# Alternating two streams of row gathers, one by one in place of four and four

## The chip, the cores and the metric

The kernel runs on one core of a Trainium2 chip. The metric is the device time of one execution in microseconds; a time quoted for a kernel is the median of its runs, and a profile shows one execution.

## What is computed

One layer of a hybrid decoder on 512 prompt tokens and 8 decode tokens: a modulated norm, one wide input projection, sliding-window attention with sinks, a pooling mixer, gated branches and an output projection; then a product-key retrieval of experts. The change touches only the last part:

```python
def peer_ffn(h, w_q, sub_keys, u_tab, v_tab):
    ...                       # 8 heads: top 16 of 128 x 128 keys -> 128 (expert, gate) pairs a token
    def block(args):          # 128 tokens a block
        hb, eb, gb = args
        act = jax.nn.gelu(jnp.einsum('td,thkd->thk', hb, u_tab[eb]))
        return jnp.einsum('thk,thkd->td', gb * act, v_tab[eb])
    ...
```

Each token needs 128 rows of the table u and 128 rows of the table v, of 1024 float32 each. Row numbers depend on the data.

## The kernel before

The program has one instruction stream for each engine, with semaphores between them written out by hand. Up to about 600 us it does the mixer, the attention and the projections; from there to the end it does the expert part, whose first steps still lie beside the query projection and the routing.

The prompt is 4 blocks (NB) of 128 tokens, one token on each partition. A block has 128 slots, four of them (GS) a step: 32 steps (STEPS) a block, 128 in all, each numbered n. One gather on POOL (an indirect DMA, L459) fetches for one slot one row for each of the 128 tokens, 512 KB, on POOL's DMA queue. A step needs four gathers of u rows and four of v rows:

- **u.** When all four have landed, DVE runs four multiply-and-sum reductions (L946) of u rows with h, adds one to `u_used`, and after ACT's GELU (L606) multiplies with the gates (L951). ACT scales four diagonal matrices by these coefficients (L610).
- **v.** When all four have landed and the diagonals are ready, PE adds eight products of a diagonal with half a tile of v rows into two banks of psum; in float32 each shows as two matmuls, so a step is 16 matmuls of L1338. Then it adds one to `v_used`.

u rows and v rows have eight buffers each, two sides of four; step n uses side n % 2. POOL may issue u of step n when DVE is done with step n-2, and v of step n when PE is done with step n-2 (L456; the counters begin at AHEAD = 2). Each side of each table has one landing semaphore, which counts all four gathers. POOL's loop (L464 to L474) issues the four u gathers of step n and then the four v gathers of step n-1. Everything that POOL issues goes in program order, and a wait holds all that is behind it. Other waits in this loop (`routed`) are for the row numbers.

DVE also routes block b+1 between the steps of block b (top-k, index arithmetic). A last part does the 8 decode tokens with 16 more gathers (L481).

Of the kernel before, what the change touches and what calls it, by code (L numbers as in the profile page):

```python
# [30 lines left out]
NB = T // P  # L31
# [20 lines left out]
GS = 4  # L52
# [119 lines left out]
def decoder_layer(nc, x_prompt, x_sample, cache_k, cache_v, state_pool, c_prompt, c_sample, norm1_g,  # L172
                  norm2_g, w_ada, b_ada, w_in, q_norm_g, k_norm_g, attn_sinks, w_pool, pool_scale,
                  w_branch_attn, w_branch_pool, w_out, peer_wq, peer_subkeys, peer_u, peer_v, consts,
                  y_prompt, y_sample, k_win_p, v_win_p, pool_p, k_win_s, v_win_s, pool_s):
    plan = bank_plan()
    order = {key: i for i, (key, _) in enumerate(plan)}
    taker = dict(plan)
    turn = {}
# [6 lines left out]
    content_before = [max((j for j in range(i) if bank_of[j] == bank_of[i]), default=None) for i in range(len(plan))]  # L186
    chunks = weight_chunks()
    chunk_at = {key: i for i, (key, _) in enumerate(chunks)}

    def sem(name):  # L190
        return nc.alloc_semaphore(name)
# [15 lines left out]
    u_landed = [sem(f"u_landed_half{i}") for i in range(2)]  # L207
    v_landed = [sem(f"v_landed_half{i}") for i in range(2)]
# [4 lines left out]
    u_used, v_used = sem("u_used"), sem("v_used")  # L213
# [8 lines left out]
    def at(off, n, a=None):  # L222
        v = arena[:, off:off + n]
        return v if a is None else v.rearrange("p (a b) -> p a b", a=a)

    def take(n):
        top[0] += n
        assert top[0] <= AR, top[0]
        return top[0] - n
# [63 lines left out]
    eidx = at(take(NB * SLOTS), NB * SLOTS, NB).bitcast(I32)  # L293
# [26 lines left out]
    u_rows = [at(o_ring + i * D, D) for i in range(2 * GS)]  # L320
    v_rows = [at(o_ring + (2 * GS + i) * D, D) for i in range(2 * GS)]
# [8 lines left out]
    def wait_filled(eng, key):  # L330

        eng.wait_ge(bank_filled, order[key] + 1)
# [15 lines left out]
    STEPS = SLOTS // GS  # L348
# [9 lines left out]
    def _(sp):  # L358
# [14 lines left out]
        for i, (key, _) in enumerate(chunks):  # L373
            if i >= RING:
                wait_filled(sp, chunks[i - RING][1])
            r = ring[i % RING]
            wide = r.rearrange("p (k n) -> p k n", k=8)
            if key[0] == "ada":
                src, dst = wad[:, :, key[1] * 512:(key[1] + 1) * 512], wide
            elif key[0] in starts:  # L380
                c0, n = starts[key[0]]
                src, dst = win[:, :, c0:c0 + n], wide[:, :, 0:n]
            elif key[0] == "gate":
                c0 = 1280 + key[1] * 512
                src, dst = win[:, :, c0:c0 + 512], wide
            elif key[0] == "wo":
                src, dst = w_out[0].rearrange("(k p) n -> p k n", p=P)[:, :, key[1] * 512:(key[1] + 1) * 512], wide
            elif key[0] == "wb":
                src, dst = w_branch_pool[0].rearrange("(k p) n -> p k n", p=P), r.rearrange("p (k n) -> p k n", k=4)
            else:  # L390
                dst = r.rearrange("p (k n) -> p k n", k=4)
                for kv in range(KV):
                    half = w_branch_attn[0, kv * G * HD:(kv + 1) * G * HD, :].rearrange("(j e) n -> e j n", j=G)
                    sp.dma_start(dst[kv * HD:(kv + 1) * HD], half).then_inc(w_loaded[i % RING], 8 * 2)
                continue
            sp.dma_start(dst, src).then_inc(w_loaded[i % RING], 16)
# [21 lines left out]
    @block.gpsimd  # L418
    def _(pool):
        pool.dma_start(gqk[:, 0, :], q_norm_g[0:1, :].broadcast_to((P, HD))).then_inc(small_loaded, 16)  # L420
        pool.dma_start(gqk[:, 1, :], k_norm_g[0:1, :].broadcast_to((P, HD))).then_inc(small_loaded, 16)
        pool.dma_start(sinks, attn_sinks[0:1, :].broadcast_to((P, HEADS))).then_inc(small_loaded, 16)
        for kv in range(KV):
            pool.dma_start(sinks4[0:G, kv:kv + 1],
                           attn_sinks[0, kv * G:(kv + 1) * G].rearrange("(j o) -> j o", o=1), allow_slow_non_contiguous=True).then_inc(small_loaded, 16)
        pool.dma_start(wpool, w_pool[0].rearrange("g c e -> c g e")).then_inc(small_loaded, 16)
        pool.dma_start(k0[0:S, :], cache_k[0, :, 0].rearrange("b h e -> b (h e)")).then_inc(small_loaded, 16)
        pool.dma_start(kc[:, P:], consts[:, P:]).then_inc(consts_loaded, 16)

        pool.wait_ge(qk_normed, 1)  # L430
        pool.dma_start(k_win_p[0, 0].rearrange("t h e -> t (h e)"), zqk[:, NB - 1, 512:640]).then_inc(windows_stored, 16)  # L431
        pool.dma_start(v_win_p[0, 0].rearrange("t h e -> t (h e)"), zv[:, NB - 1, :]).then_inc(windows_stored, 16)
        pool.dma_start(pool_p[0, 0], zp[P - HIST:P, NB - 1, :]).then_inc(windows_stored, 16)

        wait_filled(pool, ("d", 1))
        pool.dma_start(pext[0:HIST * S, :], state_pool[0].rearrange("b r c -> r b c")).then_inc(tail_loaded, 16)
        pool.dma_start(pext[HIST * S:P, :], zp[0:S, NB, :]).then_inc(tail_loaded, 16)
        pool.wait_ge(tail_loaded, 32)
        pool.dma_start(pool_s[0].rearrange("b r c -> r b c"), pext[S:P, :]).then_inc(windows_stored, 16)

        wait_filled(pool, ("gate", 2 * C - 1, 1))
        for cache, tile, new in ((cache_k, ktile, zqk[0:S, NB, 512:640]), (cache_v, vtile, zv[0:S, NB, :])):
            pool.dma_start(tile[0:WIN - 1], cache[0, :, 1:WIN].rearrange("b s h e -> s b (h e)")).then_inc(cache_loaded, 16)  # L443
            pool.dma_start(tile[WIN - 1:WIN], new).then_inc(cache_loaded, 16)
        pool.wait_ge(cache_loaded, 64)
        pool.dma_start(k_win_s[0].rearrange("b s h e -> s b (h e)"), ktile).then_inc(windows_stored, 16)
        pool.dma_start(v_win_s[0].rearrange("b s h e -> s b (h e)"), vtile).then_inc(windows_stored, 16)
        wait_filled(pool, ("y", PG - 1, 1))
        pool.dma_start(v0[0:1], cache_v[0:1, :, 0].rearrange("o b h e -> o b (h e)")).then_inc(oldest_v_loaded, 16)
        pool.wait_ge(merged_ready, 2 * C)  # L450
        pool.dma_start(sk_rows, peer_subkeys[0].rearrange("h c n e -> n (h c) e")).then_inc(subkeys_loaded, 16)  # L451
        wait_filled(pool, ("ada", 11))
        def gather(table, buf, used, landed, n):

            b, k, side = n // STEPS, n % STEPS, n % 2
            pool.wait_ge(used, n + 1)  # L456
            for i in range(GS):
                slot = k * GS + i
                pool.indirect_dma_start(  # L459
                    out=buf[side * GS + i], out_offset=None, in_=table[0],  # L460
                    in_offset=bass.IndirectOffsetOnAxis(ap=eidx[:, b, slot:slot + 1], axis=0),
                ).then_inc(landed[side], 16)

        for n in range(NB * STEPS):  # L464
            if n < OVER * TURN and n % TURN == 0:
                pool.wait_ge(routed, n // TURN + 1)
            elif n == OVER * TURN:
                pool.wait_ge(routed, OVER + 1)
            elif n == EARLY * TURN:
                pool.wait_ge(routed, OVER + 2)  # L470
            gather(peer_u, u_rows, u_used, u_landed, n)
            if n:
                gather(peer_v, v_rows, v_used, v_landed, n - 1)
        gather(peer_v, v_rows, v_used, v_landed, NB * STEPS - 1)  # L474

        pool.wait_ge(sample_routed, 1)
        for table, buf, used, landed in ((peer_u, u_rows, u_used, [sample_u_landed[t // GS] for t in range(S)]), (peer_v, v_rows, v_used, sample_v_landed)):
            for q in range(2):
                pool.wait_ge(used, AHEAD + NB * STEPS - 1 + q)
                for t in range(q * GS, (q + 1) * GS):  # L480
                    pool.indirect_dma_start(out=buf[t], out_offset=None, in_=table[0],  # L481
                                            in_offset=bass.IndirectOffsetOnAxis(ap=idx_s[:, t:t + 1], axis=0)).then_inc(landed[t], 16)
        pool.wait_ge(windows_stored, 16 * 6)
# [965 lines left out]
```

## Time and profile before

| | us |
|---|---|
| median of 3 runs (2167.91 to 2173.15) | 2167.99 |
| profiled execution | 2177.73 |
| its span, first to last instruction | 2175.9 |
| DVE reductions, L946, 512 | 597.8 |
| POOL gathers of u, L459, 512 | 664.2 |
| POOL gathers of v, L459, 512 | 494.2 |
| PE matmuls, L1338, 2048 | 1043.7 |

Engines: PE is TensorE, PEld its weight loads, DVE is VectorE, ACT is ScalarE, POOL is GpSimd. "arena" is the one tensor that holds all of the core's on-chip memory. A row of the **timeline** has the start in us, the duration in us, engine, line, operation, what it writes and reads, how many instructions are merged in the row and, in brackets, the idle time before it with what ended it; "issue" means that nothing in the profile was waited for. A row of **waits** has engine and line, what was waited for, and the sum in us, the number and the longest of these waits. A row of **windows** has the stretch, its length, each engine's busy time with its number of instructions, then the granted share of PE's full clock, the DMA engines' busy share and GB/s. A row of **lines** groups instructions: count, busy us, mean ns of one, and the idle time before them.

### The profile page before, as it was taken

What the parts mean: (1) busy time and instruction counts of PE and PEld (TensorE: products, weight loads), DVE (VectorE), ACT (ScalarE), POOL (GpSimd) and SP (SyncE); (2) the same over time, 40 slices, a digit from 0 to 9 for tenths busy, and PEclk for the clock granted to TensorE, in tenths of its full rate; (3) what the DMA queues carried; (4) which work ended last, traced back from release to release, by engine and by line L of the source; (5) the groups of instructions that cost most, each with busy time, mean ns of one, the idle gap of its engine ahead of it and who ended that gap; (6) DMA issues with size and microseconds to landing.
All of it is one profiled execution on the core that took longest, in us unless ns stands there. A gap on an engine that the chain in (4) does not pass through costs nothing.

```text
span 2175.9 us, 16338 instructions
## 1 busy us (share of the span) xinstructions
PE 1705.3 (78%) x4907; PEld 881.3 (41%) x4907; DVE 1077.1 (50%) x2685; ACT 369.0 (17%) x988; POOL 1200.8 (55%) x1066
## 2 busy tenths in 40 slices
PE   6999990999989997777676666776776777777778
PEld 2458740868556653223222222322332332223222
DVE  3012210423356678885665565665566565443443
ACT  2013430101122111111111111111111111111111
POOL 0000011000055557777777777777777778777774
PEclk9999995899999998898989899889888888988999
DMA  8222142032289889999999999999999999999996
GB/s 297 78 78 81 48 98 78 20 135 78 87 310 328 303 283 372 354 371 360 370 370 352 361 364 356 374 367 354 362 361 370 356 359 348 365 357 356 372 357 266
DMA packets 196404, 612.37 MB, mean 281 GB/s; under 512 B 21808, under 2 KB 39508, under 8 KB 196218
## 3 DMA queue, kind: packets, MB, share of 16 engines
q0 software_dynamic: 155216, 551.61, 68.7%
q1 hardware_dynamic: 41130, 60.04, 8.4%
q8 instruction: 30, 0.49, 0.1%
q14 instruction: 28, 0.23, 0.0%
HBM read 607.78 MB, written 3.59 MB: 281 GB/s over the span
## 4 chain that ended last, share of the span: by engine, by line
POOL 48%; PE 31%; issue 16%; DMA 3%; DVE 2%; ACT 0%; SPq 0%; DVEq 0%; ACTq 0%; POOLq 0%
POOL arena L459 48%; PE psum L1090 18%; PE psum L1338 4%; PE psum L1152 4%; DMA arena<-arena 1%; DMA arena<-in_peer_v,arena 1%; DMA arena<-in_x_sample 1%; POOL arena L443 1%; PE psum L1416 1%; PE psum L1322 1%; ACT arena L492 0%; PE psum L1179 0%; DVE arena L946 0%; PE psum L1405 0%; PE psum L1251 0%
## 5 line engine op out<-in xcount | busy, mean ns | idle before, releaser
L1338 PE MATMUL psum<-arena 128*128 128x512 f32 x2048 | 1043.7, 668 | 377.6 <-DMA arena<-in_peer_v,arena 368.3
L459 POOL DMA_INDIRECT arena<-in_peer_u,arena x512 | 664.2, 1297 | 347.6 <-issue 151.7
L946 DVE CUSTOM_DVE_ANT_0 arena<-arena 128x1024 f32<-128x1024 f32 x512 | 597.8, 1222 | 468.5 <-DMA arena<-in_peer_u,arena 467.6
L1338 PEld LDWEIGHTS psum<-arena 128*128 128x128 f32 x2048 | 426.8, 214 | 983.2 <-issue 868.0
L459 POOL DMA_INDIRECT arena<-in_peer_v,arena x512 | 494.2, 965 | 159.5 <-issue 155.7
L1090 PE MATMUL psum<-arena 128*128 128x260 f32 (+2 forms) x1812 | 449.2, 408 | 10.9 <-ACT arena L492 8.0
L1090 PEld LDWEIGHTS psum<-arena 128*128 128x128 f32 (+1 forms) x1812 | 320.2, 180 | 129.5 <-issue 78.5
L610 ACT ACTIVATE arena<-arena 128x128 f32<-128x128 f32 x512 | 163.5, 390 | 267.1 <-DVE arena L951 267.1
L606 ACT ACTIVATE arena<-arena 128x4 f32<-128x4 f32 x128 | 26.3, 205 | 901.8 <-DVE arena L946 901.8
L492 ACT ACTIVATE arena<-psum 128x512 f32<-128x512 f32 (+9 forms) x181 | 76.1, 451 | 498.4 <-PE psum L1090 286.6
L431 POOL DMA_DIRECT2D out<-arena x1 | 0.6, 561 | 179.5 <-DVE arena L745 179.5
L1152 PE MATMUL psum<-arena 128*128 128x512 f32 (+3 forms) x240 | 88.6, 530 | 1.6 <-DVE arena L708 1.6
L1152 PEld LDWEIGHTS psum<-arena 128*128 128x128 f32 (+1 forms) x240 | 40.9, 172 | 48.5 <-issue 44.0
L962 DVE COPY arena<-psum 128x512 f32<-128x512 f32 x16 | 11.0, 690 | 73.4 <-PE psum L1322 73.2
L756 DVE SCALAR_TENSOR_TENSOR arena<-psum,arena 128x512 f32<-128x512 f32 (+1 forms) x16 | 9.2, 619 | 70.2 <-PE psum L1179 70.0
L1241 PE MATMUL psum<-arena 128*128 128x128 f32 x8 | 2.0, 428 | 51.1 <-DMA arena<-arena 51.1
L946 DVE DVE_READ_ACCUMULATOR2_ANT arena<- 128x1 f32 x512 | 41.5, 81 | 0.0
L451 POOL DMA_DIRECT2D arena<-in_peer_subkeys x1 | 1.2, 1172 | 71.9 <-DVE arena L818 71.9
L443 POOL DMA_DIRECT2D arena<-in_cache_k x1 | 6.7, 6696 | 60.3 <-PE psum L1201 60.3
L688 DVE TENSOR_TENSOR arena<-psum,arena 128x36 f32<-128x36 f32 x12 | 2.4, 196 | 75.2 <-PE psum L1116 75.2
L951 DVE TENSOR_TENSOR arena<-arena 128x4 f32<-128x4 f32 x128 | 21.2, 166 | 35.9 <-issue 17.9
L858 DVE FIND_INDEX8 arena<-arena 128x8 uint32<-128x128 f32 (+3 forms) x99 | 32.6, 329 | 0.0
(197 smaller groups left out, 817.6 us busy)
## 6 DMA issues: line engine op xcount, KB each, us to landing
arena<-in_w_ada SPq DMA_DIRECT2D x12, 2048.0 KB, 8.9
arena<-in_w_in SPq DMA_DIRECT2D x6, 2048.0 KB, 7.7
arena<-in_peer_u,arena POOLq DMA_INDIRECT x520, 6.2
arena<-in_peer_v,arena POOLq DMA_INDIRECT x520, 6.2
arena<-in_peer_wq SPq DMA_DIRECT2D x16, 512.0 KB, 8.9
arena<-in_w_out SPq DMA_DIRECT2D x2, 2048.0 KB, 13.7
arena<-in_x_prompt SPq DMA_DIRECT2D x4, 512.0 KB
arena<-in_w_branch_attn SPq DMA_DIRECT2D x2, 1024.0 KB, 20.6
```

What stands on the lines that cost most here:

```text
L443: pool.dma_start(tile[0:WIN - 1], cache[0, :, 1:WIN].rearrange("b s h e -> s b (h e)")).then_inc(cache_loaded, 16)
L459: pool.indirect_dma_start(out=buf[side * GS + i], out_offset=None, in_=table[0], in_offset=bass.IndirectOffsetOnAxis(ap=eidx[:, b, slot:sl ...
L492: ins = act.activation(out, in_, f, **kw)
L606: act.activation(gelus[:, side, :], acts[:, side, :], ACT.Gelu_apprx_tanh).then_inc(gelu_done, 1)
L610: ins = act.activation(diags[:, side * GS + i, :], ident, ACT.Copy, scale=coefs[:, side, i:i + 1])
L858: dve.max_index(i[:, 0:8], v[:, 0:8], s)
L946: ins = dve.tensor_tensor_reduce(rows_i, rows_i, h2n[:, b, :], 1.0, 0.0, ALU.mult, ALU.add, acts[:, side, i:i + 1])
L1090: ins = pe.matmul(out, a, b, start=(n == 0), stop=(n == len(pairs) - 1))
L1152: ins = pe.matmul(o, hT[:, k, cols(b)], wt[:, k, 0:n], start=(k == 0), stop=(k == C - 1))
L1322: ins = pe.matmul(o[:, b * P:(b + 1) * P], pq[:, m % 2, b * P:(b + 1) * P], skT[m], start=True, stop=True)
L1338: ins = pe.matmul(psum[:, 2 * (b % 2) + h, :], diags[:, side * GS + i, :], v_rows[side * GS + i][:, h * 512:(h + 1) * 512], start=False, s ...
L1416: ins = pe.matmul(psum[0:S, 4 + h, :], coef_s[:, t * S:(t + 1) * S], v_rows[t][:, h * 512:(h + 1) * 512], start=(t == 0), stop=(t == S - 1 ...
```

## The change

POOL's loop issues the same gathers with the same waits in another order: u gather i of step n and v gather i of step n-1 in turn, i from 0 to 3. The wait for u's buffers stands ahead of the first u gather, the wait for v's buffers now ahead of the first v gather, which is the second gather of the step. The last iteration has v gathers alone.

```diff
-        def gather(table, buf, used, landed, n):
-
-            b, k, side = n // STEPS, n % STEPS, n % 2
-            pool.wait_ge(used, n + 1)
-            for i in range(GS):
-                slot = k * GS + i
-                pool.indirect_dma_start(
-                    out=buf[side * GS + i], out_offset=None, in_=table[0],
-                    in_offset=bass.IndirectOffsetOnAxis(ap=eidx[:, b, slot:slot + 1], axis=0),
-                ).then_inc(landed[side], 16)
-
-        for n in range(NB * STEPS):
+        def gather(table, buf, landed, n, i):
+
+            slot = n % STEPS * GS + i
+            pool.indirect_dma_start(
+                out=buf[n % 2 * GS + i], out_offset=None, in_=table[0],
+                in_offset=bass.IndirectOffsetOnAxis(ap=eidx[:, n // STEPS, slot:slot + 1], axis=0),
+            ).then_inc(landed[n % 2], 16)
+
+        for n in range(NB * STEPS + 1):
...
-            gather(peer_u, u_rows, u_used, u_landed, n)
-            if n:
-                gather(peer_v, v_rows, v_used, v_landed, n - 1)
-        gather(peer_v, v_rows, v_used, v_landed, NB * STEPS - 1)
+            if n < NB * STEPS:
+                pool.wait_ge(u_used, n + 1)
+            for i in range(GS):
+                if n < NB * STEPS:
+                    gather(peer_u, u_rows, u_landed, n, i)
+                if n and i == 0:
+                    pool.wait_ge(v_used, n)
+                if n:
+                    gather(peer_v, v_rows, v_landed, n - 1, i)
```

## Rows read from the trace of the kernel before

**Rows 1.** The page: the chain that ended last, share of the span by engine.

```profile
POOL 48%; PE 31%; issue 16%; DMA 3%; DVE 2%; ACT 0%; SPq 0%; DVEq 0%; ACTq 0%; POOLq 0%
```

**Rows 2.** Waits of POOL, 881 to 2104 us (all of them).

```profile
POOL arena L459 <- issue: 256.2, 841, 0.3
```

**Rows 3.** Windows, 881.19 to 2091.62 us, POOL.

```profile
881.19:2091.62 1210.43, 956.98 (x832) 0.89 0.97 362
```

**Rows 4.** Timeline of POOL, 1490 to 1520 us: gathers of u and of v.

```profile
1495.11 0.94 POOL L459 DMA_INDIRECT arena<-in_peer_v,arena  x1 [0.30 <-issue]
...
1501.52 0.94 POOL L459 DMA_INDIRECT arena<-in_peer_u,arena  x1 [0.30 <-issue]
...
1507.75 1.76 POOL L459 DMA_INDIRECT arena<-in_peer_u,arena  x1 [0.30 <-issue]
1509.81 1.98 POOL L459 DMA_INDIRECT arena<-in_peer_u,arena  x1 [0.31 <-issue]
1512.10 0.94 POOL L459 DMA_INDIRECT arena<-in_peer_u,arena  x1 [0.30 <-issue]
...
1514.59 0.94 POOL L459 DMA_INDIRECT arena<-in_peer_v,arena  x1 [0.30 <-issue]
...
1519.57 0.94 POOL L459 DMA_INDIRECT arena<-in_peer_u,arena  x1 [0.30 <-issue]
```

**Rows 5.** Lines of POOL, 881 to 2104 us: gathers by table.

```profile
L459 POOL DMA_INDIRECT arena<-in_peer_u,arena x421 | 572.5, 1360 | 128.3 <-issue 128.3
L459 POOL DMA_INDIRECT arena<-in_peer_v,arena x420 | 395.9, 943 | 127.9 <-issue 127.9
```

**Rows 6.** Timeline of DVE, 1507 to 1515 us: one step's reductions and its coefficients.

```profile
1507.47 1.23 DVE L946 CUSTOM_DVE_ANT_0 arena<-arena 128x1024 f32<-128x1024 f32 x1 [3.73 <-DMA arena<-in_peer_u,arena]
...
1508.62 1.22 DVE L946 CUSTOM_DVE_ANT_0 arena<-arena 128x1024 f32<-128x1024 f32 x1
...
1510.91 1.22 DVE L946 CUSTOM_DVE_ANT_0 arena<-arena 128x1024 f32<-128x1024 f32 x1
...
1514.76 0.17 DVE L951 TENSOR_TENSOR arena<-arena 128x4 f32<-128x4 f32 x1 [0.26 <-issue]
```

**Rows 7.** Timeline of PE, 910 to 2130 us: steps, the first and the last.

```profile
910.10 7.13 PE L1338 MATMUL psum<-arena 128*128 128x512 f32 x16 [2.72 <-DMA arena<-in_peer_v,arena]
...
1502.11 8.82 PE L1338 MATMUL psum<-arena 128*128 128x512 f32 x16 [3.74 <-DMA arena<-in_peer_v,arena]
1512.64 7.13 PE L1338 MATMUL psum<-arena 128*128 128x512 f32 x16 [1.71 <-DMA arena<-in_peer_v,arena]
...
2096.70 8.83 PE L1338 MATMUL psum<-arena 128*128 128x512 f32 x16 [4.72 <-DMA arena<-in_peer_v,arena]
...
2120.70 9.02 PE L1338 MATMUL psum<-arena 128*128 128x512 f32 x16 [5.11 <-DMA arena<-in_peer_v,arena]
```

**Rows 8.** Line L459, 881 to 2104 us: from a gather's issue to its landing.

```profile
DMA to landing us min/median/max: 5.1/6.2/8.9
```

**Rows 9.** Timeline of ACT, 1510 to 1520 us: one step's diagonals.

```profile
1514.96 1.28 ACT L610 ACTIVATE arena<-arena 128x128 f32<-128x128 f32 x4 [2.58 <-DVE arena L951]
```

**Rows 10.** Timeline of POOL, 2095 to 2150 us: the last step's first v gather.

```profile
2129.99 1.27 POOL L459 DMA_INDIRECT arena<-in_peer_v,arena  x1 [3.82 <-PE psum L1338]
```

**Rows 11.** Windows of 5 us, POOL: clock, DMA share, GB/s.

```profile
1497.00:1502.00 5.00, 4.09 (x4) 1.00 1.03 419
1502.00:1507.00 5.00, 3.78 (x5) 0.66 0.95 350
...
1512.00:1517.00 5.00, 3.76 (x4) 1.00 0.90 311
```

**Rows 12.** Windows, 700 to 800 us, PE, PEld, DVE, ACT and POOL.

```profile
700.00:800.00 100.00, 100.00 (x382) 66.49 (x381) 67.56 (x191) 18.58 (x53) 49.63 (x52) 1.00 0.87 304
```

**Rows 13.** Waits of POOL, 600 to 881 us.

```profile
POOL arena L459 <- DVE arena L946: 63.0, 13, 9.9
```

## The prediction

> **What bounds the kernel now.** I read the page first: POOL leads the chain that ended last, with 48% of the span at L459, the line that issues the gathers, and another 16% is "issue"; PE has 31% [rows 1]. L459 does its work after 600 us, so the second view is what POOL waited for in the long stage that repeats, between 881 and 2104 us: nothing. 841 gaps sum to 256.2 us, none longer than 0.3 us [rows 2]: the engine's own gap between two gathers. POOL issues back to back and sets the pace. From 881.19 to 2091.62 it issues 832 gathers, 104 steps of eight, in 1210.43 us [rows 3]: 11.64 us per step.
>
> A gather costs 0.94 us and the gap 0.30 us, 1.245 us between starts [rows 4], so eight cost 9.96 us. The other 1.68 us per step is gathers that last longer: in the grouped view u gathers average 1360 ns and v gathers 943 ns [rows 5], which is (421 x 0.42 + 420 x 0.003)/105 = 1.69 us per step. The timelines show why. At 1507.75 a u gather takes 1.76 us and the next, at 1509.81, 1.98 us [rows 4]; in these microseconds DVE runs the four reductions of L946, from 1507.47, one every 1.145 us [rows 6]. Take 0.94 us off each gather's end and it could go on at 1508.57 and 1510.85, just where the second and the fourth reduction begin. So a gather that starts while a reduction runs is held to that reduction's end. One that follows the last reduction takes 0.94 us [rows 4].
>
> How far is the rest from taking over? A step's buffers come free again when DVE (u) or PE (v) has worked on the step two before it. The last v gather of one step starts at 1495.11 [rows 4], PE begins that step at 1502.11 (7.00 us later) and works 8.82 us, to 1510.93 [rows 7]; the gather that reuses the buffers starts at 1514.59 [rows 4]. **Slack: 3.66 us.** For u: last gather 1501.52 [rows 4], reductions 1507.47 to 1512.13 [rows 6], reuse at 1519.57 [rows 4], 7.4 us. Both cover POOL now. The two slacks are what the change spends.
>
> **The change, part by part.** It removes and adds no gather, no byte and no instruction on another engine. POOL's program has the same waits, with the v wait in another place.
>
> (1) *The order of issue.* Now, from the last u gather of a step to the first u gather that reuses the buffers there are thirteen places in POOL's queue (v v v v, u u u u, v v v v, u); afterwards ten (v, a whole step of eight, u). For v the same: thirteen (u4 v4 u4, then v) becomes ten (a whole step, u, v). The other gap, from the first to the last gather of one table in a step, grows from three places to six.
>
> (2) *The u wait.* Ten places: 10 x 1.245 + 1.69 (one step's holds) = 14.14 us. Needed: landing (median 6.2 us from issue [rows 8]), four reductions 4.66 us [rows 6], about 0.3 us for release: 11.2 us. It still fits, with 3 us to spare. Cost nothing; the cover is those 3 us. The later u rows also reach PE later through the coefficients. From a last u gather at 1501.52 [rows 4] the coefficients start at 1514.76 [rows 6] and ACT ends its four scalings at 1516.24 [rows 9]: 14.7 us. From the last u to the last v of a step there will be nine places, 9 x 1.245 + 1.69 = 12.9 us, plus the landing: 19.1 us. v rows still come last. Nothing.
>
> (3) *The v wait.* Ten places again, 14.14 us, against 19.48 us in the example [rows 4] (thirteen places and two steps' holds; 19.57 us by the means). The slack shrinks by 5.43 us. It is needed for landing, PE's step and 0.27 us of release (PE's step from 2120.70 ends at 2129.72 [rows 7], the waiting gather starts at 2129.99 [rows 10]: the one place where POOL is held by PE today). PE's steps between the first and the last row of [rows 7] are of three kinds: of 104, 46 take 7.13 us, 38 take 8.5 to 8.83, and 20 take 9 or more, up to 10.2. The difference is the clock, 0.89 on the mean there [rows 3]: in the step from 1502.11, which PE began after 3.74 us of idle time and needed 8.82 us for [rows 7], the granted share is 0.66 from 1502 to 1507; in the 7.13 us step from 1512.64, after 1.71 us of idle time [rows 7], it is 1.00 [rows 11]. The two levels are 1.2 and 2.4 GHz, and the lower one follows the longer idle time. Read as in the example, slack averages 5.96, 4.29 and 3.22 us in the three kinds. Less 5.43: **+0.53, -1.14 and -2.21 us.** POOL will stand at the first v gather after every PE step that ran partly at the low clock. Behind that wait are queued three u gathers and the whole rest of the step, so DVE and the DMA queue get everything later.
>
> (4) *The sum.* 38 x 1.14 + 20 x 2.21 = 88 us if every shortfall counted in full; with those of the fast steps that fall short, 89. Two things take some back. A stall also moves the next step's first v gather, whose own PE step was issued before it: going through the 104 steps in order, with each stall deducted from the next step's shortfall, leaves 72 us. And while POOL stands, the DMA queue drains, so the next rows land sooner: landing spans 5.1 to 8.9 us, median 6.2 [rows 8]. I take 0.4 us, about a third of the way from median to minimum (an estimate): the same pass with 5.03 us in place of 5.43 gives about 55 us, **0.53 us per step.** Bounds of this term: 30 us (1.1 us sooner, the minimum landing), 89 us (nothing given back).
>
> (5) *Elsewhere.* Before about 780 us PE is the bound (busy 100.00 of 100 us from 700 to 800 [rows 12]); POOL waits there for DVE, 63.0 us in 13 waits [rows 13], and a later u row or an earlier v wait lies in that idle time. From 800 to 881 DVE has a backlog from routing; a stall of POOL is again covered by rows that landed early. 0, at most 5 us. The tail keeps its order (v rows of the last step alone), 0 to 2 us. I take 0 for both.
>
> Sum: 55 us. The profiled run took 2177.73 us (span 2175.9), which would become about 2233; against the median of 2167.99 it is 2223 us.
>
> **The rivals.** *A, same time.* Memory would be the limit, and order is then free. The stage moves 362 GB/s on the mean at a DMA share of 0.97 [rows 3], so little seems to be left; the time would stay 2168. Against it: from 1497 to 1502, after a run of gathers that nothing held, the rate is 419; from 1512 to 1517, after two held ones, 311 [rows 11]. The rate follows POOL, not the other way round. The Trainium skill ("DMA: Bandwidth & Descriptors", Specifications) puts the HBM limit of one core at about 358 GB/s; by that rule the stage would be full and A the likeliest, but the trace's 419 GB/s in 5 us differs from it, and the measurement decides. Half of A's chance is another road to the same end: the slow steps of PE follow each other, so that stalls are mostly given back, the landing comes down to its minimum, and holds shrink by what is left. 2168.
>
> *B, faster.* The holds shrink. A step's holds depend on when, after DVE's first reduction, POOL's next gather starts: at 0.28 us (1507.75 against 1507.47 [rows 4, 6]) they are 0.82 + 1.04. Started at about 1.1 us only one hold of 1.04 would be left, 0.65 us less per step, 68 us over 105 steps. Together with the stalls of (4): 2168 + 55 - 68 = 2155. It decides only if nearly every step shifts to that best phase: holds must fall by more than 0.53 + 0.06 us per step. Against it: in the cyclic order of eight, the gather that meets the reductions stays the fifth after a step's last u gather, and the landing of that gather sets DVE's start in both versions. The phase has no reason to improve.
>
> *C, much slower.* POOL's stalls lengthen PE's idle time, and every PE step runs at the low clock in its first half: 10.1 us. Then two steps need landing 6.1 + 10.1 + 0.27 + six places from first to last v gather (6 x 1.245 + 1.69 = 9.16) = 25.6 us, 12.8 per step, +1.17 us: 2168 + 123 = 2291. For it: low clock follows idle time, which is 4.7 to 5.1 us before the 8.83 and 9.02 us steps at the end [rows 7]. Against: the idle share grows only by half a microsecond in 11.6.
>
> That the order is not what it says can hardly be: POOL issues in program order on one queue, as the rows of today show four and four [rows 4].
>
> **How the numbers follow.** Forecast (v turnaround stalls POOL, +20 to +94 us) 0.70; C 0.08; A 0.10; B 0.12. A measurement of this kernel tells about 0.3% (6.5 us) from no change. Slower by more than that: 0.70 + 0.08 = 0.78; within: 0.10; faster: 0.12. Range: low 2165, just under A; high 2262, all 89 us of (4) and 5 us of (5); B and most of C, 0.2, are left out.
>
> **What would show it.** In the changed profile, POOL's waits must show a new row, L459's successor waiting for PE L1338, in some 40 to 60 of the 105 steps, about 1 us each, and no row for DVE L946 after 881 us beyond a few. Gathers of both tables should be long in equal parts, with holds still near 1.7 us per step. u and v landings should be a little under 6.2 us, and the DMA rate about 345 GB/s. PE's idle time before L1338 should grow by some 50 us. I am wrong if POOL waits for PE almost nowhere (then slack (3) is misread), or if it waits but holds fall as much (B).

## The result, and the profile after

The changed kernel takes 2273.52 us (median of 4 runs, 2271.14 to 2283.51) against 2168.37 us: a ratio of 1.0488, 95% interval 1.0454 to 1.0523, 105 us slower. The forecast was 2223, the range 2165 to 2262. The sign came as forecast, and so did the place of the new wait; the size was about twice the forecast one.

The page of the changed kernel, its chain (share of the span by engine), to be read against [rows 1]. Line numbers moved: the gathers are L456, the reductions L948, PE's products L1340.

```profile
PE 52%; POOL 20%; DMA 18%; issue 9%; ACT 1%; DVE 0%; SPq 0%; ACTq 0%; DVEq 0%; POOLq 0%
```

POOL had 48% and PE 31%. The chain now leads from POOL through a landing to PE and back to POOL: 18% of it is DMA, which had 3%. What POOL waits for between 881 and 2200 us, against [rows 2]:

```profile
POOL arena L456 <- issue: 240.6, 789, 0.3
POOL arena L456 <- PE psum L1340: 126.8, 58, 3.8
```

The second row is new. Each such wait contains the 0.30 us gap that every gather has, so POOL stands (waits beyond that gap) 126.8 - 58 x 0.30 = 109 us. The same 104 steps in one window, against [rows 3]:

```profile
887.16:2181.28 1294.12, 933.26 (x832) 0.85 0.93 338
```

A step went from 11.64 to 1294.12/104 = 12.44 us, and the rate from 362 to 338 GB/s. The gathers by table, against [rows 5]:

```profile
L456 POOL DMA_INDIRECT arena<-in_peer_v,arena x423 | 485.1, 1147 | 238.2 <-PE psum L1340 126.8 <-issue 111.3
L456 POOL DMA_INDIRECT arena<-in_peer_u,arena x424 | 466.4, 1100 | 129.3 <-issue 129.3
```

Holds, the time by which gathers last longer than 0.94 us, now fall on both tables: (485.1 + 466.4 - 847 x 0.94)/106 = 1.47 us a step, 0.22 less than before.

Where the time went, by the two profiled executions (spans 2269.3 and 2175.9, 93.4 us apart): up to the first u gather of step 21 it is 887.16 - 881.19 = 6.0 us, in the 104 steps 1294.12 - 1210.43 = 83.7, behind them (2269.3 - 2181.28) - (2175.9 - 2091.62) = 3.7. The medians differ by 105 and not by 93, since the profiled execution of before lay 9.4 us above its median and that of after 2.4 below its own.

Three steps on PE, and POOL at the same time, show the pattern. PE's timeline:

```profile
1563.12 9.93 PE L1340 MATMUL psum<-arena 128*128 128x512 f32 x16 [7.62 <-DMA arena<-in_peer_v,arena]
1573.34 7.13 PE L1340 MATMUL psum<-arena 128*128 128x512 f32 x16 [0.29 <-DMA arena<-in_peer_v,arena]
1589.46 8.71 PE L1340 MATMUL psum<-arena 128*128 128x512 f32 x16 [8.99 <-DMA arena<-in_peer_v,arena]
```

POOL's timeline:

```profile
1573.32 1.82 POOL L456 DMA_INDIRECT arena<-in_peer_v,arena  x1 [3.52 <-PE psum L1340]
...
1585.21 0.94 POOL L456 DMA_INDIRECT arena<-in_peer_v,arena  x1 [0.30 <-issue]
...
1598.44 1.92 POOL L456 DMA_INDIRECT arena<-in_peer_v,arena  x1 [2.18 <-PE psum L1340]
```

And the granted clock in the first two of these steps (windows; the share of the full clock is the third number from the end):

```profile
1563.00:1573.30 10.30, 9.93 (x16) 0.72 1.02 409
1573.30:1580.50 7.20, 7.13 (x16) 1.00 0.55 168
```

PE ends at 1573.05, and 0.27 us later the gather that stood for 3.2 us starts. The step that follows begins 0.29 us after the last one, at full clock, takes 7.13 us, and its gather at 1585.21 waits for nothing. The one after that starts after 8.99 us of idle time and takes 8.71 us; POOL stands again, at 1598.44. In 56 of 104 steps POOL stands, mostly every second one.

### The profile page after: what moved, and what is told of

Read it like the earlier page. It is cut to its first block, busy times and chain, and to the rows that moved or that the text cites. A ratio compares the mean times of both kernels' runs of the same rounds, so it can differ in the third digit from the quotient of the medians.

```text
span 2269.3 us, 16338 instructions
## 1 busy us (share of the span) xinstructions
PE 1717.5 (76%) x4907; PEld 888.0 (39%) x4907; DVE 1078.7 (48%) x2685; ACT 368.9 (16%) x988; POOL 1177.2 (52%) x1066
## 4 chain that ended last, share of the span: by engine, by line
PE 52%; POOL 20%; DMA 18%; issue 9%; ACT 1%; DVE 0%; SPq 0%; ACTq 0%; DVEq 0%; POOLq 0%
PE psum L1340 26%; POOL arena L456 20%; PE psum L1092 18%; DMA arena<-in_peer_v,arena 16%; PE psum L1154 4%; DMA arena<-arena 1%; DMA arena<-in_x_sample 1%; POOL arena L443 1%; PE psum L1418 1%; PE psum L1324 1%; ACT arena L494 0%; PE psum L1181 0%; PE psum L1407 0%; PE psum L1253 0%; PE psum L1133 0%
## 5 line engine op out<-in xcount | busy, mean ns | idle before, releaser
L1340 PE MATMUL psum<-arena 128*128 128x512 f32 x2048 | 1057.8, 676 | 459.8 <-DMA arena<-in_peer_v,arena 447.9
L948 DVE CUSTOM_DVE_ANT_0 arena<-arena 128x1024 f32<-128x1024 f32 x512 | 598.1, 1223 | 565.6 <-DMA arena<-in_peer_u,arena 564.6
L1340 PEld LDWEIGHTS psum<-arena 128*128 128x128 f32 x2048 | 433.9, 218 | 1072.3 <-issue 923.9
L456 POOL DMA_INDIRECT arena<-in_peer_u,arena x512 | 557.0, 1088 | 343.8 <-issue 151.9
L456 POOL DMA_INDIRECT arena<-in_peer_v,arena x512 | 577.9, 1129 | 282.8 <-PE psum L1340 148.2
L948 DVE DVE_READ_ACCUMULATOR2_ANT arena<- 128x1 f32 x512 | 41.5, 81 | 0.0
```

The source lines that it names most:

```text
L456: pool.indirect_dma_start(out=buf[n % 2 * GS + i], out_offset=None, in_=table[0], in_offset=bass.IndirectOffsetOnAxis(ap=eidx[:, n // STEP ...
L948: ins = dve.tensor_tensor_reduce(rows_i, rows_i, h2n[:, b, :], 1.0, 0.0, ALU.mult, ALU.add, acts[:, side, i:i + 1])
L1340: ins = pe.matmul(psum[:, 2 * (b % 2) + h, :], diags[:, side * GS + i, :], v_rows[side * GS + i][:, h * 512:(h + 1) * 512], start=False, s ...
```

## The experiments

My theory after the result: POOL stands because v's turn-around (landing, the whole PE step, release) no longer fits into the ten places of its queue. The rivals: alternation itself costs (mixed or later landings); and, for the size, that the clock feeds back.

| kernel | us | ratio to the kernel before, run beside it, 95% interval |
|---|---|---|
| changed kernel | 2273.52 | 1.0454 to 1.0523 |
| wait moved alone, four and four | 2230.38 | 1.0225 to 1.0273 |
| alternating, release by row | 2171.03 | 0.9980 to 1.0016 |
| alternating, six fillers | 2246.97 | 1.0303 to 1.0347 |
| alternating, three fillers | 2261.35 | 1.0384 to 1.0454 |
| eleven places | 2206.11 | 1.0131 to 1.0168 |
| twelve places | 2168.88 | 0.9974 to 1.0015 |
| nine places | 2407.98 | 1.1069 to 1.1122 |
| four and four, release by row | 2170.11 | 0.9992 to 1.0021 |
| the same, h from psum in 48 steps | 2099.68 | 0.9654 to 0.9697 |
| alternating, release by row, h from psum | 2103.65 | 0.9675 to 0.9720 |

**The wait without the alternation.** The order of before, with the v wait moved forward (the edit is shown against the changed kernel):

```diff
 for i in range(GS):
     if n < NB * STEPS:
         gather(peer_u, u_rows, u_landed, n, i)
     if n and i == 0:
         pool.wait_ge(v_used, n)
-    if n:
-        gather(peer_v, v_rows, v_landed, n - 1, i)
+for i in range(GS if n else 0):
+    gather(peer_v, v_rows, v_landed, n - 1, i)
```

> The four and four order of the kernel before; only the wait for v's buffers is put behind the first u gather, where the changed kernel has it. From the last v gather of a step to the wait there are again ten places, and six more from the gather behind the wait to the next last v gather, as in the changed kernel. Theory (the place of the v wait and PE's turn-around cost the time, not the alternation): about the changed kernel's 2273 us, 2255 to 2290, with some 55 waits of POOL for PE that sum to 105 to 130 us. Rival (alternation itself costs: later and mixed landings, other holds): 2165 to 2185.

It took 2230 us: 59 us slower than before with no alternation at all, but 43 less than I expected. POOL's waits between 881 and 2160 us:

```profile
POOL arena L456 <- PE psum L1340: 109.9, 64, 4.1
```

That is 109.9 - 64 x 0.30 = 91 us of standing, near the changed kernel's 109. What differs is where POOL stands. POOL's timeline and, below it, DVE's:

```profile
1419.80 1.01 POOL L456 DMA_INDIRECT arena<-in_peer_u,arena  x1 [0.30 <-issue]
1422.80 1.84 POOL L456 DMA_INDIRECT arena<-in_peer_u,arena  x1 [1.99 <-PE psum L1340]
```

```profile
1420.31 1.22 DVE L948 CUSTOM_DVE_ANT_0 arena<-arena 128x1024 f32<-128x1024 f32 x1 [0.32 <-DMA arena<-in_peer_u,arena]
1421.46 1.22 DVE L948 CUSTOM_DVE_ANT_0 arena<-arena 128x1024 f32<-128x1024 f32 x1
```

POOL stands up to 1422.80 while the reductions run, in which its gathers would in part have been held anyway. Added up over both timelines, 90 of 91 us of standing lie inside reductions here, and 13 of 109 in the changed kernel. Holds fall accordingly, to 1.28 us a step (from 1.69, 43 us over 105 steps): 91 - 43 = 48 us in the stage, and about 10 us more ahead of it. Standing that lies wholly inside the reductions still costs about half. So a stall's price is what is left after the holds it covers; both my theory and its rival had missed that.

**Release by row.** PE adds to `v_used` after each row's two products, and POOL waits for one row (the other waits on `v_used`, scaled by four, are left out):

```diff
-    if n and i == 0:
-        pool.wait_ge(v_used, n)
     if n:
+        pool.wait_ge(v_used, (n - 1) * GS + i + 1)
         gather(peer_v, v_rows, v_landed, n - 1, i)
...
     for i in range(GS):
         for h in range(2):
             ins = pe.matmul(...)
-    ins.then_inc(v_used, 1)
+        ins.then_inc(v_used, 1)
```

> The changed kernel, in which PE adds to v_used after each row's two products (four times a step) and POOL waits before each v gather for that row's buffer alone; all other waits on v_used are scaled. The first v gather then needs landing 6.4 + a quarter of PE's step, 2.2, + 0.27 = 8.9 us of the 14 us that ten places take. Theory (the wait for the whole PE step): POOL no longer waits for PE, 8 x 1.245 + holds of 1.45 to 1.7 us give 11.4 to 11.65 us a step: 2145 to 2175. Rival (alternation itself): it stays over 2230.

2171 us, the time of before (interval 0.9980 to 1.0016), in full alternation. POOL's waits for PE between 881 and 2200 us are 55 of 0.3 us, the gap itself; below it the window of the 104 steps, 11.6 us each as before:

```profile
POOL arena L456 <- PE psum L1339: 16.8, 55, 0.3
```

```profile
881.68:2086.00 1204.32, 950.63 (x833) 0.89 0.97 364
```

The release by row alone changes nothing in the order of before (2170 us, under "The holds"). So the whole loss is the wait for the end of PE's step. Alternation, later u rows and mixed landings cost nothing that can be measured.

**Places.** Three more orders, with the v wait always ahead of the first v gather:

```diff
-u v u v u v u v     # changed kernel, ten places
+u u v u v u v v     # eleven
+u u u v u v v v     # twelve
+v u v u v u u v     # nine
```

> Order u u v u v u v v: v begins one place later than in the changed kernel, so eleven places, 1.245 us more, from a last v gather to the wait. Theory (shortfall against places): each of some 55 stalls of 1.88 us shrinks by up to 1.245 us, some vanish: 30 to 50 us of waits, 2185 to 2220. Rival (alternation itself, same amount of mixing): within 15 us of the changed kernel, 2258 to 2288.

> Order u u u v u v v v: twelve places from a last v gather to the wait, two more than in the changed kernel, 12 x 1.245 + 1.6 = 16.5 us. In the changed kernel a stalled step's turn-around was 6.45 + 9.14 + 0.27 = 15.9 us. Theory (shortfall against places): only PE steps of over 9.7 us fall short, by under 1 us each: waits below 15 us, 2168 to 2188. Rival (each place of alternation costs the same share, 35 us): about 2203.

> Order v u v u v u u v: nine places to the wait, one fewer than in the changed kernel, and seven from first to last v gather. Theory: POOL stands in nearly every pair of steps, and a pair lasts turn-around 15.9 + 7 x 1.245 + 1.45 = 26.0 us against the changed kernel's 24.8: 0.6 us more a step, 2315 to 2350. Rival (the loss is used up at ten places, a floor set by the landing): within 15 us of 2273.

POOL's waits for PE from 881 us, in eleven, twelve and nine places:

```profile
POOL arena L456 <- PE psum L1340: 52.1, 46, 3.6
```

```profile
POOL arena L456 <- PE psum L1340: 5.4, 6, 2.4
```

```profile
POOL arena L456 <- PE psum L1340: 233.9, 54, 6.1
```

Net of the gaps: 38, 4 and 218 us (with nine places seven more waits, about 29 us net, stand under "issue"); the times are 2206, 2169 and 2408. Thirteen, twelve, eleven, ten and nine places cost 0, 1, 35, 105 and 240 us against the runs of before beside them: a threshold, then a curve that gets steeper. Twelve and eleven came as the shortfall against places says. Nine took 58 us more than the top of its range. PE's timeline there:

```profile
1584.07 9.93 PE L1340 MATMUL psum<-arena 128*128 128x512 f32 x16 [8.75 <-DMA arena<-in_peer_v,arena]
1594.74 7.13 PE L1340 MATMUL psum<-arena 128*128 128x512 f32 x16 [0.74 <-DMA arena<-in_peer_v,arena]
1611.72 9.77 PE L1340 MATMUL psum<-arena 128*128 128x512 f32 x16 [9.85 <-DMA arena<-in_peer_v,arena]
```

PE's steps pair up more sharply: a long idle time, a step at the low clock in part, one right behind it. A pair lasts 27.3 us (1584.07 to 1611.72 is 27.7), where I had 26.0. The steps on which POOL waits average 9.5 us against the changed kernel's 9.1, and the release takes 0.78 us in place of 0.27 (1594.00 to 1594.78, the start of the gather that waited) there. In five of the seven waits under "issue" the gather starts 3.3 us after PE's end; why, and the rest, I have not taken apart.

**Fillers.** Matmuls of zeros ahead of PE's steps, to keep the clock up:

```diff
+for i in range(0 if isinstance(it, int) else 6):     # or 3
+    pe.matmul(psum[:, 2 * (b % 2) + i % 2, :], zeros, zeros[:, 0:1].broadcast_to((P, 512)),
+              start=False, stop=False, skip_group_check=True)
 pe.wait_ge(v_landed[side], ...)
```

> The changed kernel with six matmuls of zeros ahead of each PE step (from step 16 on), before its wait for v rows, so that PE is not idle long: 2.6 us at full clock. They add zero to the sums. Theory with a feedback through the clock (a stalled step is one that begins after 5.9 us of idle time at the low clock and takes 9.1 us): all steps take 7.13 us, the turn-around 6.4 + 7.13 + 0.27 = 13.8 us fits into ten places, the waits fall below 30 us in sum: 2165 to 2205. Rival (the clock is a by-product, the stalls come from late landing): steps shorten, waits stay above 70 us, 2230 or more.

> The changed kernel with three matmuls of zeros ahead of each PE step from step 16 on (1.3 us at full clock), in place of the six that themselves put PE's start off by 1 us. Theory (feedback through the clock): more PE steps of 7.13 us than the 40 of 104, start not put off, waits below 60 us: 2200 to 2250. Rival (the clock is a by-product): 2262 or more with the waits over 100 us.

2247 and 2261 us. The edit reaches less than both expectations say: a turn that is not part of a longer loop gets no fillers, and the trace has 1056 passes over zeros, twelve in each of 88 steps, from step 16 to 103. The last 24 steps ran without:

```profile
L1337 PE MATMUL psum<-arena x1056: 592/592/595, 856.5 to 1917.7; 128*128 128x512 f32 x176
```

The run with six could not tell the theories apart, because I had mispriced the filler. PE's timeline:

```profile
1499.65 5.33 PE L1337 MATMUL psum<-arena 128*128 128x512 f32 x12
1504.83 7.03 PE L1343 MATMUL psum<-arena 128*128 128x512 f32 x16
1511.69 5.33 PE L1337 MATMUL psum<-arena 128*128 128x512 f32 x12
1516.86 7.03 PE L1343 MATMUL psum<-arena 128*128 128x512 f32 x16
```

Six fillers are twelve float32 passes, 5.33 us: here PE never rests and is itself the bound, at 12.0 us a step. All 83 steps from 21 to 103 take 7.13 us, and POOL stands 41 us in them, where the changed kernel has 88. With three (2.7 us) 49 of these 83 steps take 7.13 us, against 32, and POOL stands 70 us; with the last steps it is 96 us against 109:

```profile
POOL arena L456 <- PE psum L1343: 112.0, 54, 3.9
```

2261 lies just under the rival's bound and just outside the theory's range. The interval (1.0384 to 1.0454) only touches the changed kernel's. So the clock has a share in the size, about 12 us by the medians, with a third of the slow steps gone where the fillers ran (34 left of 51); how much all of it is, these runs do not settle.

**The holds.** The release by row alone, in the order of before, and then with h read from psum in blocks 1 and 2 from their third turn on:

```diff
-ins = dve.tensor_tensor_reduce(rows_i, rows_i, h2n[:, b, :], ...)
+ins = dve.tensor_tensor_reduce(rows_i, rows_i, h_psum(b) if from_psum[0] else h2n[:, b, :], ...)
...
+act.wait_ge(y_ready, b)                  # ACT, after the block's first turn
+for i in range(2):
+    ins = act.activation(h_psum(b)[:, i * 512:(i + 1) * 512], h2n[:, b, i * 512:(i + 1) * 512], ACT.Copy)
+ins.then_inc(h_in_psum, 1)
...
+dve.wait_ge(h_in_psum, b)                # DVE, ahead of the third turn
+from_psum[0] = True
```

> The order of the kernel before with PE's release row by row and nothing else, the control for e8_rows_psum. POOL does not wait for PE in the kernel before, so nothing can be gained: 2162 to 2175. Rival (the release itself gave part of e8_rows_psum's 68 us): below 2155.

> The order of the kernel before, with PE's release row by row, and in blocks 1 and 2 from their third turn on (48 steps) the reductions read h from psum, where ACT copies it after the block before is finished, in place of the on-chip memory that POOL reads too. Theory (a gather is held while a reduction reads two operands from that memory): in these 48 steps gathers take 0.94 us, 8 x 1.245 = 9.96 us a step or 10.3 where the DMA queue sets the pace, against 11.64: 2168 - 48 x 1.34 = 2104, 2090 to 2125. Rival (the hold has another cause, any reduction): 2160 to 2180.

> The alternating order with PE's release row by row, and in blocks 1 and 2 from their third turn on h read from psum, as in e8_rows_psum, which has the four and four order (2099.7 us). In those 48 steps the DMA queue set the pace in e8_rows_psum: 410 GB/s, landing 9.3 us. Theory (order is free where the queue is full; u's turn-around of 9.3 + 4.66 + 0.3 = 14.3 us exceeds ten places, 12.45, but POOL's standing only drains the queue): 2095 to 2115. Rival (ten places bind u as they bound v): 48 steps x 0.9 us more, 2135 or above.

The control takes 2170 us, no change. With h in psum it is 2100 us, 3.2% faster than before and the best of all. POOL's timeline in that kernel, then DVE's:

```profile
1206.98 0.94 POOL L469 DMA_INDIRECT arena<-in_peer_u,arena  x1 [0.30 <-issue]
1208.22 0.94 POOL L469 DMA_INDIRECT arena<-in_peer_u,arena  x1 [0.30 <-issue]
1209.47 0.93 POOL L469 DMA_INDIRECT arena<-in_peer_v,arena  x1 [0.31 <-PE psum L1365]
1210.70 0.94 POOL L469 DMA_INDIRECT arena<-in_peer_v,arena  x1 [0.30 <-issue]
```

```profile
1207.30 1.22 DVE L966 CUSTOM_DVE_ANT_0 arena<-arena,psum 128x1024 f32<-128x1024 f32 x1 [3.20 <-DMA arena<-in_peer_u,arena]
1208.45 1.22 DVE L966 CUSTOM_DVE_ANT_0 arena<-arena,psum 128x1024 f32<-128x1024 f32 x1
1209.59 1.22 DVE L966 CUSTOM_DVE_ANT_0 arena<-arena,psum 128x1024 f32<-128x1024 f32 x1
```

The reductions last as long as before, and they hold no gather: in 44 such steps 345 of 352 gathers take up to 1.0 us, and the other seven, at most 1.27, lie beside a TENSOR_TENSOR of the routing on DVE. A stretch of block 1 and one of block 3, which still reads h from the on-chip memory (windows, POOL):

```profile
1150.00:1300.00 150.00, 112.92 (x121) 0.92 1.03 410
...
1850.00:2000.00 150.00, 118.39 (x104) 0.89 0.97 363
```

121 gathers in 150 us instead of 104, 410 GB/s instead of 363. The landing grows from 6.2 to 9.3 us (median): 121 gathers of 512 KB in 150 us ask for 423 GB/s and the queue moves 410, so it fills. But POOL still hardly stands: a step takes 10.04 us, where eight gathers with their gaps cost 9.96. So the queue does not yet set the pace. The alternating order costs little there (2104 us, the intervals overlap). The theory for that run gave the right time, but u's turn-around did not grow to 14.3 us, because the landing stayed near 7.6 us. It is 12.1 to 12.3 us and the release, about the 12.45 us of its ten places, and POOL stands some 8 us in 44 steps.

## Why the prediction was wrong in size

- **What bounds the kernel** stands: POOL back to back, with holds by the reductions. That was only read from the timelines; the kernel with h in psum shows it.
- **(1) and (2), order and u wait:** right. Between 881 and 2200 us POOL never waits for DVE, and releasing v by row, with u still at ten places, gives the time of before.
- **(3), the v wait:** right in place and count. Forecast were 40 to 60 waits of about 1 us for PE; there are 58, of 1.9 us net.
- **(4), the sum, is the step that failed.** 55 us of standing were forecast, 109 measured (105 of them behind the PE steps of the same 104). Three terms of it were mis-sized:
  - I took 0.4 us off for a queue that drains. In the changed kernel the landing to PE's start averages 6.45 us on the steps on which POOL waits, as before (6.48): six gathers have followed a stall by then. Without the 0.4 us the pass gives 73 us.
  - I named the release of 0.27 us in (3) and did not deduct it: slack ends at PE's end, the gather starts 0.27 later. With it the pass gives 85.
  - I kept the holds at 1.69 us inside the ten places. They fell by 0.22, so ten places without a stall take 13.9 us and not 14.14. With that the pass gives 95.

  The rule that a stall is credited to the next step did not fail. In the changed kernel's own timelines the shortfalls add up to 126 us, and 21 of them lie under the stall before; from the rows of before, with the release, the rule gives back 25. The last 10 us stay open. There are more slow steps, 64 of 104 in place of 58, but they are not longer (9.1 us on the mean in both). They are spread otherwise: on POOL's waits the PE step averages 9.1 us after 6.0 us of idle time, on the others 7.4 after 1.8. Only the runs with fillers bear on that, and they settle the clock's share no further than "some".
- **Holds, kept at 1.69 us:** they fell to 1.47, 23 us in the kernel's favour. The stage then loses 109 - 23 = 86 us, and 83.7 are measured. So fewer holds lengthen the standing and pay back more than that.
- **(5), elsewhere:** forecast 0, at most 7 us; it is 6.0 ahead of step 21 (12 waits for PE before 881 us, forecast as covered) and 3.7 behind. The other 12 us of the 105 are the two profiled executions' places against their medians, which no term of the sum could hold.
- **The range** ended at 2262 because "nothing given back" was taken as the worst case of a sum that lacked the release and those 12 us.
- **Rivals.** A fell: in the kernel with h in psum the same memory gives 410 GB/s over 150 us, where it had 362. The Trainium skill's limit of about 358 GB/s for one core ("DMA: Bandwidth & Descriptors", Specifications) is therefore no bound here, and the measurement decides. A's other road, stalls mostly given back, fell too: 21 of 126 us were. B's mechanism is real, holds fall a little, but far less than the stalls. C, all steps at 10.1 us, did not come: the mean step went from 8.23 to 8.33 us, and 40 steps of 104 still take 7.13.

## What to carry to other kernels

When an order of issue is changed, count for each buffer set the places in the queue from its last fill to its next one; compare the slowest turn-around, not the mean one, with the time these places take. With eleven places the mean turn-around of v (15.0 us) is shorter than the places without a stall (15.3 us), and POOL still stands 38 us: there the spread of the turn-arounds, up to 17.0 us, makes it stand. With ten places even the mean, 14.9 us, exceeds the 13.9 us of the places. A wait can be made cheap from either side: release buffers one by one, which took all of the loss away here, or let it fall where the waiting engine would be held anyway, which left 59 of the 105 us.

## What the runs showed of the hardware

A POOL gather, which reads its row numbers from the on-chip memory, took up to 1.05 us longer (1.99 in place of 0.94) while DVE ran a reduction with both inputs there, and 0.94 us in the rows above where one of the inputs was in psum. The Trainium skill states this rule ("SBUF — State Buffer", Who interferes with whom): DVE's second input comes through the read interface that it shares with GpSimd. The trace agrees: 1.69 us of holds a step with both inputs there, 0.01 in 44 steps with one of them in psum. It is worth 68 us from 48 of 128 steps, where the change lost 105 on all of them.
